# Loading rows in runs of four: MLP down and seven output blocks, with strided weight columns

## The reference

```python
# even layer, odd layer: x = x + rmsnorm(mixer(rmsnorm(x)) @ w_out);  y = concat(heads) gated, then:
y @ w_out                                   # even: 1536 x 1024, odd: 1024 x 1024
...
def sq_relu_mlp(h, w1, w2):
    return jnp.square(jax.nn.relu(h @ w1)) @ w2     # w1 1024 x 4096, w2 4096 x 1024
...
# third block: attention and gated convolution, merged, then the output projection
merged = gate_a * (y_a @ w_pa[l]) + gate_b * (y_b @ w_pb[l])
x = x + ga1[:, None, :] * (merged @ w_o[l])         # w_o 1024 x 1024
x = x + ga2 * hierarchical_moe(h2, ...)             # 32 experts, top 2 of one group
```

## Time and profile before

| | |
|---|---|
| median of 3 runs | 1546.45 us (1545.59 to 1546.57) |
| the profiled execution | 1544.59 us, its span 1542.8 us |
| TensorE matmul / weight load busy | 1301.6 us / 706.0 us |
| VectorE / ScalarE / GpSimd busy | 438.7 / 197.8 / 74.0 us |
| mean granted TensorE clock | 0.924 |
| moved by DMA | 376.72 MB in 93462 packets, 244 GB/s over the span |

### The profile page before, as it was taken

How to read it: one execution, slowest core, us unless ns; L and a number is a source line. 1 busy time by engine, 2 the same in 40 slices (tenths; PEclk the granted TensorE clock), 3 DMA queues, 4 the chain that set the end, 5 groups by cost and what they waited for, 6 DMA issues and landing times.

```text
span 1542.8 us, 12328 instructions
## 1 busy us (share of the span) xinstructions
PE 1301.6 (84%) x5308; PEld 706.0 (46%) x5308; DVE 438.7 (28%) x614; ACT 197.8 (13%) x280; POOL 74.0 (5%) x77
## 2 busy tenths in 40 slices
PE   7899998999999997999999999998746646636646
PEld 3455546886444453888444445444312212212212
DVE  3355122456441532346544220214100000000002
ACT  2321111111010321111001122102100000000000
POOL 0126001000000000000001100000000000000000
PEclk9999998999999999999999999999878868878878
DMA  9433433885453314587553533456699999999996
GB/s 333 144 109 127 146 118 101 301 300 188 167 187 107 132 62 173 182 298 248 182 192 115 194 133 109 149 232 257 284 428 427 428 428 428 428 428 428 427 424 224
DMA packets 93462, 376.72 MB, mean 244 GB/s; under 512 B 6976, under 2 KB 7520, under 8 KB 81504
## 3 DMA queue, kind: packets, MB, share of 16 engines
q1 hardware_dynamic: 92696, 373.80, 62.8%
q0 software_dynamic: 576, 2.10, 0.4%
q10 hardware_dynamic: 136, 0.04, 0.0%
HBM read 374.88 MB, written 1.05 MB: 244 GB/s over the span
## 4 chain that ended last, share of the span: by engine, by line
PE 74%; DMA 19%; DVE 3%; SPq 1%; issue 1%; ACT 1%; POOL 0%; POOLq 0%; DVEq 0%; ACTq 0%
PE PS L610 23%; PE PS L777 15%; PE PS L787 12%; DMA weights<-in_w 10%; DMA proj_rows<-in_w 9%; PE PS L635 8%; PE PS L998 5%; PE PS L1029 3%; PE PS L581 1%; PE PS L691 1%; SPq L406 1%; PE PS L962 1%; PE PS L747 1%; PE PS L970 1%; PE PS L821 0%
## 5 line engine op out<-in xcount | busy, mean ns | idle before, releaser
L610 PE MATMUL PS<-weights,normalised 128*128 128x512 f32 x832 | 365.1, 598 | 2.4 <-DVE normalised L1345 2.2
L610 PEld LDWEIGHTS PS<-weights,normalised 128*128 128x128 f32 x832 | 158.1, 192 | 196.6 <-issue 196.6
L998 PE MATMUL PS<-weights,arena 128*32 128x512 f32 x512 | 142.0, 717 | 115.4 <-DMA weights<-in_w 82.3
L777 PE MATMUL PS<-normalised,weights 128*128 128x256 f32 x1024 | 224.0, 382 | 1.7 <-DVE normalised L1345 1.7
L777 PEld LDWEIGHTS PS<-normalised,weights 128*128 128x128 f32 x1024 | 196.1, 192 | 29.4 <-DVE normalised L1345 2.3
L787 PE MATMUL PS<-weights,arena 128*128 128x512 f32 x384 | 167.4, 592 | 0.0
L635 PE MATMUL PS<-weights,arena 128*128 128x512 f32 x288 | 125.1, 594 | 5.4 <-issue 4.5
L998 PEld LDWEIGHTS PS<-weights,arena 128*32 128x32 f32 x512 | 36.6, 129 | 187.0 <-issue 160.3
L787 PEld LDWEIGHTS PS<-weights,arena 128*128 128x128 f32 x384 | 73.0, 190 | 91.0 <-issue 90.9
L1817 DVE TENSOR_TENSOR arena<-arena,PS 128x512 f32<-128x512 f32 x8 | 8.4, 1047 | 294.8 <-PE PS L998 294.8
L998 PE MATMUL PS<-arena 128*32 128x512 f32 x208 | 72.3, 723 | 22.8 <-DMA proj_rows<-in_w 22.8
(11 more groups left out here) (283 smaller groups left out, 1091.2 us busy)
## 6 DMA issues: line engine op xcount, KB each, us to landing
weights<-in_w SPq DMA_DIRECT2D x41, 2048.0 KB, 26.7
weights<-in_mlp_w SPq DMA_DIRECT2D x32, 2048.0 KB, 7.8
arena<-in_w SPq DMA_DIRECT2D x21, 2048.0 KB, 24.8
proj_rows<-in_w SPq DMA_DIRECT2D x20, 2048.0 KB, 25.0
proj_rows<-in_w_ada SPq DMA_DIRECT2D x12, 2048.0 KB, 8.2
weights<-in_ev_w_in SPq DMA_DIRECT2D x10, 2048.0 KB, 8.0
weights<-in_w_in SPq DMA_DIRECT2D x10, 2048.0 KB, 7.9
normalised<-in_w SPq DMA_DIRECT2D x10, 2048.0 KB, 24.4
```

The lines of the kernel that those rows point to most:

```text
L610: last = mm(PS[:, 2 * (n % 2) + tt, :], HT[:, k, tt * P:(tt + 1) * P], wn(s)[:, k, :], start=(k == 0), stop=(k == KT - 1))
L777: last = mm(PS[:, 4 + 2 * h + j // 2, (j % 2) * T:(j % 2 + 1) * T], wn(s)[:, k, j * P:(j + 1) * P], HT[:, k, :], start=(k == 0), stop=(k = ...
L998: last = mm(PS[CAP * x:CAP * (x + 1), 4 + kind, :], XG[:, k, CAP * x:CAP * (x + 1)], w[:, k, :], start=(k == 0), stop=(k == KT - 1), tile_ ...
```

## The change

The seven output blocks (`ev_w_out`, `od_w_out`, `w_o`) and the sixteen `w2` blocks are loaded so that partition p holds rows 4p to 4p + 3: one piece of 16 KB. `w_pa` and `w_pb` stay as they are. For the left operands to come in the same order, piece j must hold features j, j + 4, j + 8 and so on. So the up stage's stationary operand and the sources of the transposes take columns at a step of four fp32 values, 16 bytes.

```diff
+        def run_type(w, at):
+
+            return w[bass.ds(at, NB), :].rearrange("(p k) n -> p k n", p=P)
...
-                load(B_EV_OUT + b, k_type(A["ev_w_out"][0], b * NB))
+                load(B_EV_OUT + b, run_type(A["ev_w_out"][0], b * NB))
...
-                        load(base + b, k_type(w2, (b - NGRP) * NB))
+                        load(base + b, run_type(w2, (b - NGRP) * NB))
...
-                load(B_OD_OUT + b, k_type(A["od_w_out"][0], b * NB))
+                load(B_OD_OUT + b, run_type(A["od_w_out"][0], b * NB))
...
-                load(B_WO + b, k_type(A["w_o_2"][0], b * NB))
+                load(B_WO + b, run_type(A["w_o_2"][0], b * NB))
...
                     pe.wait_ge(sem(ready), value)
-                    quad(bank, [PR[:, tt, col + j * P:col + (j + 1) * P] for j in range(4)])\
-                        .then_inc(sem("mix_T_raw"), 1)
+                    rows = PR[:, tt, col:col + NB].rearrange("p (c j) -> p j c", j=4)
+                    quad(bank, [rows[:, j, :] for j in range(4)]).then_inc(sem("mix_T_raw"), 1)
...
                             last = mm(PS[:, 4 + 2 * h + j // 2, (j % 2) * T:(j % 2 + 1) * T],
-                                      wn(s)[:, k, j * P:(j + 1) * P], HT[:, k, :],
+                                      wn(s)[:, k, :].rearrange("p (c j) -> p j c", j=4)[:, j, :], HT[:, k, :],
                                       start=(k == 0), stop=(k == KT - 1))
...
                     c = 3072 + half * NB
-                    quad(4 + 2 * tt + half, [PR[:, tt, c + j * P:c + (j + 1) * P] for j in range(4)])\
-                        .then_inc(sem("mg_T_raw"), 1)
+                    rows = PR[:, tt, c:c + NB].rearrange("p (n j) -> p j n", j=4)
+                    quad(4 + 2 * tt + half, [rows[:, j, :] for j in range(4)]).then_inc(sem("mg_T_raw"), 1)
```

## The result

The changed kernel takes 1562.34 us (median of four runs, 1560.80 to 1563.82) against 1546.02 for the kernel before: ratio 1.0107, 95% interval 1.0092 to 1.0122. It is slower by 16.3 us, where 7.1 were forecast. The profiled execution took 1563.82 us, its span 1562.0, which is 19.2 more than the span before.

The account below looks back on a forecast made before the run. TensorE was taken as the bound, busy 84% of the span. MLP up 2.6, transposes 4.5 and loads 0 summed to 7.1 us: 1551.7 us from the profiled 1544.59, or 1553.5 against the median 1546.45; range 1545.5 to 1566.

Parts of the forecast that it names:

- The loads: 23 changed weight loads (MLP down, output blocks): nobody waits for them, so longer pieces give 0 us.
- MLP up's mechanism: MLP up's 1024 weight loads: 109.4 ns under a 216.3 ns pair, so 107 ns longer before the load bounds.
- The half-clock start of layer 0: MLP up in layer 0: its 113.22 us, against layer 1's 110.77, put down to a start at half clock.
- MLP up's price: 1024 strided weight loads in MLP up: (218.8 - 216.3) ns each, 2.6 us slower; bounds 0 and 14 us.
- a doubling: Strided weight load in MLP up takes twice 109.4 ns, 218.8 ns; likeliest case, chance 0.40.
- friction: MLP up: 2.2 ns a pair when load and matmul are equally long, from L691; would make its term 4.8 us.
- The transposes: 56 transposes with sources at stride four: each load doubled from 109 ns, 4.5 us slower in sum.
- the switch of limiter at 208.27: Four even quads of transposes at 208.27: the limiter changes from ScalarE's copies to TensorE, 1.54 us slower.
- Dearer than the slack: Rival: strided load 230 ns as L1275, bounding MLP up; 14 + 5.0 = 19 us slower, 1565.5 us; chance 0.12.
- The free stride: Rival: strided loads in MLP up and transposes stay at 109 ns; not slower, 1546.5 us; chance 0.28.
- the likeliest case: Whole kernel with every strided load doubled: 1550 to 1557 us; chance 0.40.

Follow-up runs that it names:

- the step of two: Kernel before with `w2` loaded as two neighbouring rows per partition and MLP up's weight columns at a step of two values: 1546.30 us, ratio 0.9997.
- the probe: Separate kernel of only fp32 matmul and transpose sequences, stationary operand at steps 1 to 32; at step 4, 234 ns a load start to start, 236 by division.

## Why the prediction was wrong

- **The loads.** Right: no landing was waited for before, MLP down kept its 96.1 us, packets fell to 84631 (84630 forecast), and the step of two, with pieces of 8 KB and no strided cost, stands at 0.9997.
- **MLP up's mechanism.** Right: a load of 109 ns under a pass of 216.3 has 107 ns of slack, it grew past that, and the stage turned from the matmul's pace to the load's. The half-clock start of layer 0 fits in direction: it cost 2.45 us over layer 1 before and 2.05 after, when a pair at full clock was already longer.
- **MLP up's price, the step that failed.** "I take a doubling, 218.8 ns, near the upper one" gave 2.6 us; the load measures 234 ns in the kernel and alone (236 by division), 2.14 times the 109.4, and the term is 17.7 us. Because the slack absorbs the first 107 ns, an error of 15 ns in the load (7%) became one of 15 us in the time, a factor of seven in the term. The row L1275 in the earlier trace rows had it: 0.94 ns a value gives 230 ns and 14 us; measured is (236 - 114) / 128 = 0.95. I named this row as the nearest and then took the rounder number. That it was right to 4 ns is in part luck: it is a ScalarE write at a step of 512 bytes, and no run shows that it and the weight load have a cause in common. The "friction" of 2.2 ns from L691 does not exist: L622's loads start 112 ns apart, as L691's passes do (111.6), and the kernel's 234 is the probe's 234.
- **The transposes.** Wrong the other way: 4.5 us forecast, 10 ns each measured (0.95 us for eight), at most 0.6 us over 56 and less on the path; the switch of limiter at 208.27 did not happen. I gave one price to all stationary operands. The trace of the kernel before held a hint that I did not look at: a transpose's load lasts about 140 ns, a matmul's 192 at the same shape, so one price for both was not to be taken for granted.

```profile
L1008 PEld LDWEIGHTS PS<-constants,arena x32: 138/140/143, 1100.8 to 1518.3; 128*128 128x128 f32 x32
```

- **The rivals.** "Dearer than the slack" (0.12) is what happened, at 14 + 5.0 = 19 us instead of 17.7 and almost nothing. The free stride (0.28) is refuted. The rule of the Trainium skill ("Advanced Engine Details and Errata", SBUF Cachelines) pointed the right way: at full clock two uses of a 16-byte line are nearly free (117 against 112 ns), one is not (234). The sentence of the Trainium skill's "SBUF — State Buffer", Door 1, that four fp32 may be stepped for free does not hold here; the measurement decides.
- The time lay in the range (1545.5 to 1566) only because the range was drawn to take in a rival with a chance of 0.12; it lay outside the likeliest case's own 1550 to 1557. The direction, slower, was right; the size was less than half.

## What to carry to other kernels

Where one operand load hides under another operation with little slack, price it by the nearest measured row, not by a round factor, or measure it alone first: just past the slack every nanosecond counts in full, here 1024 times. Count the 16-byte pieces that a strided fp32 operand of a TensorE matmul touches, at about 1.8 ns each, before choosing a layout for DMA's sake, and prefer pairs or groups within a piece. And check first that somebody waits for the transfer: here nobody did, and pieces of 4, 8 and 16 KB won nothing.

## What was not expected of the hardware

- An fp32 operand of a matmul with fewer than two values per 16-byte piece costs about 1.8 ns a piece, on the stationary side (steps 3 and 4, 96 and 128 pieces: 174 and 234 ns; 64 columns at step 4: 120) and on the moving side (256 pieces: 456 ns). At steps 5, 6, 16 and 32 it was 219 to 224 ns for 128 pieces, at step 8 240, at step 12 269; that is not explained.
- The pace of the load at step 4 did not follow TensorE's clock: 234 ns at 0.50 as at 1.00, where the contiguous one went from 112 to 213.
- A transpose with a source at step four costs 13 ns more (123 against 110), not 125. It is a cheap place for a permutation: in the experts it took over one that cost VectorE 0.36 us.
